# Seven products instead of eight for the seventh down chunk of two MLPs, with the recombination spread over VectorE and accumulating transfers

## What is computed

```python
h = rms_norm(x, norm_mlp[l])
x = x + jnp.square(jax.nn.relu(h @ w_up[l])) @ w_down[l]      # first block
return rms_norm(x, norm_final)

hid = jnp.square(jax.nn.relu(jnp.einsum('bsd,df->bsf', n2, w_up[l])))   # second block
mlp_out = jnp.einsum('bsf,fd->bsd', hid, w_down[l])
h = h + rms_norm_2(mlp_out, norm_mlp_post[l])
```

## Time and profile before

| | |
|---|---|
| three runs | 1566.63, 1567.47, 1567.72 us, median 1567.47 |
| the profiled execution | 1567.51 us, of which span 1565.7 us |
| granted TensorE clock | 0.999 |
| TensorE matmuls busy | 1549.0 us, 99% of the span, 7752 instructions |
| VectorE, ScalarE, GpSimd busy | 987.3, 662.7, 482.6 us |

### The profile page before, as it was taken

The page is one execution under the profiler, slowest core; times in us unless marked ns, Lnnn a source line. Parts: engine busy times, 40 slices in busy tenths (PEclk is TensorE's granted clock), DMA queues, the critical chain, the costliest instruction groups (busy, mean ns, idle before and its releaser), DMA issues.

```text
span 1565.7 us, 21038 instructions
## 1 busy us (share of the span) xinstructions
PE 1549.0 (99%) x7752; PEld 1303.1 (83%) x7752; DVE 987.3 (63%) x1188; ACT 662.7 (42%) x1092; POOL 482.6 (31%) x282
## 2 busy tenths in 40 slices
PE   8999999999999999999999999999999999999998
PEld 6888888888788888888888898988888988888886
DVE  5454876435477776876664747357356677777765
ACT  5352665244444443443533433643334453434342
POOL 2451000000037776752300000020013047767732
PEclk9999999999999999999999999999999999999999
DMA  6422136221313233215332132243334332213133
GB/s 247 150 70 79 41 108 191 79 81 54 135 54 108 108 108 107 107 55 160 89 106 83 55 95 71 92 162 105 111 124 147 135 108 102 89 45 135 67 116 120
DMA packets 44997, 164.35 MB, mean 105 GB/s; under 512 B 5584, under 2 KB 5784, under 8 KB 44272
## 3 DMA queue, kind: packets, MB, share of 16 engines
q1 hardware_dynamic: 40608, 144.82, 28.4%
q0 software_dynamic: 4304, 18.38, 3.4%
HBM read 158.89 MB, written 5.85 MB: 105 GB/s over the span
## 4 chain that ended last, share of the span: by engine, by line
PE 93%; DVE 4%; ACT 2%; DMA 1%; issue 1%; SPq 0%; DVEq 0%; ACTq 0%
PE banks L1235 29%; PE banks L1237 29%; PE banks L1236 29%; PE banks L1534 1%; PE banks L1413 1%; DVE nmax L2230 1%; DVE w_lo L1944 1%; DMA w_raw<-in_weights 1%; PE banks L1352 0%; PE banks L1596 0%; DVE banks L2229 0%; PE banks L1572 0%; PE banks L1564 0%; PE banks L1523 0%; DMA x_tok<-in_x 0%
## 5 line engine op out<-in xcount | busy, mean ns | idle before, releaser
L1235 PE MATMUL banks<-act_hi,w_hi 128*128 128x512 f32 (+1 forms) x1088 | 413.7, 380 | 3.1 <-DVE act_lo L2112 3.1
L1237 PE MATMUL banks<-act_hi,w_lo 128*128 128x512 f32 (+1 forms) x1088 | 410.3, 377 | 0.0
L1236 PE MATMUL banks<-act_lo,w_hi 128*128 128x512 f32 (+1 forms) x1088 | 410.2, 377 | 0.0
L1944 DVE TENSOR_TENSOR w_lo<-w_raw,w_hi 128x1024 fp32r<-128x1024 f32 x216 | 280.0, 1303 | 203.2 <-ACT w_hi L1632 199.8
L1632 ACT ACTIVATE w_hi<-w_raw 128x1024 fp32r<-128x1024 f32 x216 | 227.0, 1059 | 251.6 <-DMA w_raw<-in_weights 196.8
L1235 PEld LDWEIGHTS banks<-act_hi,w_hi 128*128 128x128 f32 x1088 | 204.9, 188 | 40.8 <-DVE w_lo L1944 1.6
L1237 PEld LDWEIGHTS banks<-act_hi,w_lo 128*128 128x128 f32 x1088 | 204.9, 188 | 37.7
L1236 PEld LDWEIGHTS banks<-act_lo,w_hi 128*128 128x128 f32 x1088 | 205.0, 188 | 36.4
L1235 PE MATMUL banks<-w_hi,a_hi 128*128 128x512 f32 x400 | 155.8, 389 | 0.0
L1237 PE MATMUL banks<-w_hi,a_lo 128*128 128x512 f32 x400 | 155.7, 389 | 0.0
L1236 PE MATMUL banks<-w_lo,a_hi 128*128 128x512 f32 x400 | 155.7, 389 | 0.0
(11 more groups left out here) (367 smaller groups left out, 2393.4 us busy)
## 6 DMA issues: line engine op xcount, KB each, us to landing
w_raw<-in_weights SPq DMA_DIRECT2D x216, 512.0 KB, 3.7
w_down<-in_weights SPq DMA_DIRECT2D x48, 512.0 KB, 6.4
wide<-share_dram POOLq DMA_DIRECT2D x3, 1024.0 KB, 10.2
x_tok<-in_x SPq DMA_DIRECT2D x4, 512.0 KB, 5.2
w_first<-in_weights SPq DMA_DIRECT2D x4, 512.0 KB, 8.5
x_tok<-in_x POOLq DMA_DIRECT2D x4, 512.0 KB, 5.0
x_dram<-x_tok POOLq DMA_DIRECT2D x1, 2048.0 KB, 8.1
x_tok<-x_dram POOLq DMA_DIRECT2D x1, 2048.0 KB, 8.5
```

The lines of the kernel that those rows point to most:

```text
L1235: pe.matmul(out_ap, lhs[0], rhs[0], start=start, stop=False)
L1236: pe.matmul(out_ap, lhs[0], rhs[1], start=False, stop=False)
L1237: return pe.matmul(out_ap, lhs[1], rhs[0], start=False, stop=stop)
L1944: dve.tensor_tensor(w_lo[:, slot, :], landed(kind, raw), w_hi[:, slot, :], ALU.subtract).then_inc(lo_w, 1)
```

## The change

Chunk 6 of both networks is done by seven products as well (`seven`, `last=True`), with banks 4, 6, 0, 2, 4, 6, 2 (and each one's neighbour) instead of 4 and 6 in turn. Its weights come through `w_down`, and POOL makes their block sums in up 7. The step `whole` (`sq` to `act_hi`, `act_lo` for chunk 7) moves ahead of the products; the replaced part is gone. The recombination leaves up 7: in the product stage VectorE does q6 += q1 after product 2, q7 += q6 after product 4, x12 += q6 and x12 += q5 after product 5; x21 += q7 comes right ahead of VectorE's add of tile 2, half 0, of chunk 7. The quarters x11 (+= q1) and x22 (+= q5, += q7) are left to accumulating transfers from SBUF to SBUF, 512 KB each, that POOL issues; POOL itself waits for the q5 transfer before it issues the q7 one. `load2` keeps six of its transfers and moves behind product 6's evacuation; the seventh (`row2`) is issued after product 0. The return of x in the second block goes to a buffer of its own, `x_late`, from product 0 on. VectorE waits for the transfers at tile 0 half 0 and at tile 2 half 1.

```diff
-    return name in ("w_down", "w_down_2") and row0 < FF - 2 * T
+    return name in ("w_down", "w_down_2") and row0 < FF - T
...
+        if last:
+            sums, held = None, self.count("lo_a", 4)
+            self.add("whole", held=held, sq=squared)
...
-            bank = 4 + 2 * (j % 2)
+            bank = (4, 6, 0, 2, 4, 6, 2)[j] if last else 4 + 2 * (j % 2)
...
-        s.add("whole", held=s.count("lo_a", 1), sq=s.count("sq", 0), dst="parts")
-        up(after="fold")
-        after_last()
-        steps = s.bank_steps("add", "tok", "parts", rows=4, halves=2, dst=dst)
-        go(steps, 1)
-        s.add("whole", held=s.count("lo_a", 4), sq=s.count("sq", 0), dst="act")
-        go(steps, 16)
-        s.add("unpark", ready=ready(), dst=dst)
+        up()
+        for st in s.products(dst, last=True):
+            taken = filled_by(st)
+            if st.n == 0:
+                first_out(taken)
+                s.add("unpark", ready=taken, dst=dst)
+            s.add("fold", n=st.n, ready=taken, dst=dst)
+        after_last(taken)
         last(s.bank_steps("add", "tok", "act", rows=4, halves=2, dst=dst, by_tile=True))
...
-    run_mlp("x", lambda: s.add("load2", ready=all_out()), first_end)
+    run_mlp("x", lambda taken: s.add("row2_load", ready=taken), lambda taken: s.add("load2", ready=taken), first_end)
...
             def fold(st):
...
+                q, (x11, x12, x21, x22) = sums_of[st.dst], quarters(st.dst)
+                if st.n > 0:
+                    wait_ready(dve, st.ready, None)
+                if st.n == 2:
+                    then(dve.tensor_tensor(q["q6"], q["q6"], q["q1"], ALU.add))
+                elif st.n == 4:
+                    dve.tensor_tensor(q["q7"], q["q7"], q["q6"], ALU.add).then_inc(q7_made, 1)
+                    dve.wait_ge(q7_made, FOLDED[st.dst] // 16)
+                elif st.n == 5:
+                    then(dve.tensor_tensor(x12, x12, q["q6"], ALU.add))
+                    then(dve.tensor_tensor(x12, x12, q["q5"], ALU.add))
...
+            def fold_late(dst):
...
+                x21 = quarters(dst)[2]
+                then(dve.tensor_tensor(x21, x21, sums_of[dst]["q7"], ALU.add))
...
+                    if st.rows == 4:
+                        for name in {(0, 0): ("x11",), (2, 1): ("x22_q5", "x22")}.get((st.nth, st.half), ()):
+                            dve.wait_ge(fold_in[name], FOLDED[st.dst])
                     part = dst[:, st.nth, col0:col0 + 512]
+                    if st.rows == 4 and (st.nth, st.half) == (2, 0):
+                        fold_late(st.dst)
...
+            def fold_by_dma(st):
...
+                if st.n in (1, 3):
+                    wait_ready(pool, st.ready, None)
+                if st.n == 1:
+                    pool.dma_start(x11, q["q1"], accum_op=ALU.add).then_inc(fold_in["x11"], 16)
+                elif st.n == 3 and st.dst == "y":
+                    pool.dma_start(x22, q["q5"]).then_inc(fold_in["x22_q5"], 16)
+                elif st.n == 3:
+                    pool.dma_start(x22, q["q5"], accum_op=ALU.add).then_inc(fold_in["x22_q5"], 16)
+                elif st.n == 4:
+                    pool.wait_ge(q7_made, done // 16)
+                    pool.wait_ge(fold_in["x22_q5"], done)
+                    pool.dma_start(x22, q["q7"], accum_op=ALU.add).then_inc(fold_in["x22"], 16)
```

More of the change, by code:

```diff
@@ L374, in ahead, with products @@
         return out
-    def products(self, dst, first=False):
+    def products(self, dst, first=False, last=False):
         g = self.group
@@ L387, in products @@
         squared = self.count("sq", 0)
-        sums = self.add("sums", counts={"sum_a": 4}, sq=squared, held=self.count("lo_a", 0)).sum_a
-        held = self.count("lo_a", 7)
+        if last:
+            sums, held = None, self.count("lo_a", 4)
+            self.add("whole", held=held, sq=squared)
+        else:
+            sums = self.add("sums", counts={"sum_a": 4}, sq=squared, held=self.count("lo_a", 0)).sum_a
+            held = self.count("lo_a", 7)
         for j in range(7):
-            bank = 4 + 2 * (j % 2)
+            bank = (4, 6, 0, 2, 4, 6, 2)[j] if last else 4 + 2 * (j % 2)
             banks = (bank, bank + 1)
@@ L398, in products @@
             ends.append((bank + 1, self.cell(self.fills[bank + 1] + 1, ("bank", bank + 1))))
-            yield self.add("product", banks, n=j, dst=dst, first=first, splits=splits,
+            yield self.add("product", banks, n=j, dst=dst, first=first, last=last, splits=splits,
                            units=[self.placed(self.mine[j])], held=held, of=ends, sum_a=sums, sq=squared)
-        self.last_bank = 5
+        self.last_bank = bank + 1
 def at(count, turn, plus=0):
@@ L1042, in two_blocks @@
         tile_done = sem("tile_done")
-        fold_made, parked, x_again = sem("fold_made"), sem("parked"), sem("x_again")
+        parked, x_again = sem("parked"), sem("x_again")
+        fold_in = {name: sem(f"fold_{name}") for name in ("x11", "x22_q5", "x22")}
+        q7_made = sem("q7_made")
         sq_made = sem("sq_made")
@@ L1152, in part_lo, with quarters @@
             eng.tensor_tensor(a_lo[:, j], parts[j], a_hi[:, j], ALU.subtract).then_inc(lo_a, 1)
+        def quarters(dst):
+            rows_of = {"x": x, "y": y}[dst]
+            return [rows_of[:, 2 * rows:2 * rows + 2, 512 * cols_:512 * cols_ + 512] for rows in range(2) for cols_ in range(2)]
         def copies_of(st):
@@ L1716, in handle @@
                     split(st, turn)
+                    if st.last:
+                        return
                     act.wait_ge(sq_made, at(st.sq, turn))
@@ L2030, in handle @@
                     split(st, turn)
+                elif k == "fold":
+                    fold(st)
                 elif k == "product":
@@ L2400, in handle @@
                     block_sums(pool, st, turn)
-                elif k == "product":
+                elif k == "product" and not st.last:
                     for j in (st.n - 1, st.n) if st.n == 6 else (st.n - 1,):
@@ L2405, in handle @@
                 elif k == "whole":
-                    pool.wait_ge(hi_a, at(st.held, turn, 1))
-                    if st.dst == "parts":
-                        pool.tensor_tensor(a_lo[:, 2], sq[:, 0:2, low_], a_hi[:, 2], ALU.subtract).then_inc(lo_a, 1)
-                    else:
-                        for c in range(4):
-                            pool.wait_ge(hi_a, at(st.held, turn, c + 1))
-                            pool.tensor_tensor(act_lo[:, c, :], sq[:, c, :], act_hi[:, c, :], ALU.subtract).then_inc(lo_a, 1)
+                    for c in range(4):
+                        pool.wait_ge(hi_a, at(st.held, turn, c + 1))
+                        pool.tensor_tensor(act_lo[:, c, :], sq[:, c, :], act_hi[:, c, :], ALU.subtract).then_inc(lo_a, 1)
+                elif k == "fold":
+                    fold_by_dma(st)
                 elif k == "gemm":
@@ L2467, in handle @@
                     if st.mode == "final":
-                        pool.wait_ge(fold_made, 1)
+                        for name in {0: ("x11",), 1: (), 2: ("x22_q5",), 3: ("x22",)}[st.n]:
+                            pool.wait_ge(fold_in[name], 16)
                     src = x if st.mode == "final" else y
@@ L2514, in handle @@
                         pool.dma_start(wide[p][:].rearrange("q t h -> q (t h)"), share_dram[p].partition_broadcast(P)).then_inc(wide_in[p], 16)
+            def fold_by_dma(st):
+                q, (x11, x12, x21, x22) = sums_of[st.dst], quarters(st.dst)
+                done = FOLDED[st.dst]
+                if st.n in (1, 3):
[10 more added lines that the diff above has]
+                    pool.dma_start(x22, q["q7"], accum_op=ALU.add).then_inc(fold_in["x22"], 16)
             def level(n, st):
```

51 lines of the change are left out of this document (17 added, 34 removed).

## The result

| | before | after |
|---|---|---|
| median | 1567.19 us | 1570.72 us |
| lowest and highest of 22 runs each | 1566.63 to 1568.02 | 1568.68 to 1572.42 |
| profiled execution, span | 1567.51, 1565.7 us | 1570.68, 1568.9 us |
| granted TensorE clock over the span | 0.999 | 0.997 |

The ratio is 1.0022, 95% interval 1.0016 to 1.0028: 3.5 us slower, where 1.2 us faster than these 1567.19 was predicted. It lies above the range (1569.4), so this is a miss.

What follows compares the result with a forecast made beforehand. TensorE's matmuls fill 99% of the span and bound the kernel. Against 1567.51 us: -5.44 saved, +2.7 first turn, +0.5 second turn, +0.7 at the end, -1.5 in sum, 1566.0 us; range 1563.2 to 1569.4.

Steps and rivals of the forecast that it cites:

- The saving: Chunk 6's product stages: 84 matmuls where the plain chunk has 96, saving 2.72 us per block, 5.44 in all.
- the third rival: Product stage: late loads make TensorE wait for bank 2, losing the saving there too; 1569.5 or 1567.8 us, chance 0.15.
- VectorE's backlog: Chunk 6's product stage: VectorE some 4 us behind when down 7 begins, evacuating product 6 at t near 22.3 to 23.5.
- The place of the damage: First block: six `load2` issues hold POOL from 23.5 to 26.7, ahead of its first work on tile 0.
- The x21 term: Addition at tile 2 of chunk 7: 0.5 us at the first block's second turn, 0.7 us at the program's end.
- The second block: Forecast change of the second block's time: -2.0 us.
- What the delay does in the first block: First turn, tile 0: late `load2` issues make TensorE wait 3.4 us for `h_tok`, 2.7 us added.
- I take 6.2: Accumulating 512 KB transfers between SBUF buffers: 6.2 us each, between 5.0 from below and 8.5 from above.
- the prediction's own sign: On POOL in the new profile: a wait for the q5 transfer past t = 24 would mean the second rival.
- the second rival: Slow accumulating transfers hold POOL ahead of `load2` and tile 0: 1570 us at 10.5 us each, 1574 at 12.5; chance 0.15.

Runs made afterwards that it cites:

- e10: First block as before the change, second block changed, with its x21 addition moved into the product stage behind product 6: 1564.53 us, ratio 0.9983 to before.
- e3: First block as before the change, second block as in the changed kernel: 1564.95 us, ratio 0.9986 to before.
- e8: Changed kernel with the first block's three accumulating transfers as plain copies of the same bytes: 1570.16 us, ratio 1.0017 to before.
- e1: Changed kernel with the six `load2` transfers issued behind tile 0's first addition instead of ahead of it: 1567.39 us, ratio 1.0000 to before.
- e7: Changed kernel with 22 useless matmuls (5.0 us) ahead of the first block's first turn: 1568.66 us, ratio 1.0007 to before.
- e9: e1 with 14 useless matmuls (3.2 us) ahead of the first turn: 1565.94 us, ratio 0.9993 to before.
- e2: Changed kernel with VectorE adding q7 to q5 and one transfer to x22 in place of two: 1571.51 us, ratio 1.0028 to before.
- e4: Changed kernel with the x21 addition in the product stage, behind product 6, in both blocks: 1569.87 us, ratio 1.0016 to before.
- e6: e5 with the second block's x21 addition moved behind product 6's evacuation: 1568.24 us, ratio 1.0008 to before.
- e5: e1 with tile 0 of the first block turned one half tile later, behind tile 2's first half: 1568.81 us, ratio 1.0012 to before.

## Why the prediction was wrong

**What held.** The saving: both product stages of 19.04 us, no gap, no wait for banks or weights; the third rival did not come. VectorE's backlog: product 6 evacuated at t = 23.0 to 24.3 (said: 22.3 to 23.5), three late loads and four additions being its content. The place of the damage: six issues in front of tile 0's product. The x21 term: 0.5 us at the second turn (0.52 measured), 0.7 at the end (0.76; e10 takes it away). The second block: -2.0 said, -2.2 measured alone (e3).

**The step that failed is "What the delay does in the first block", the sum of which was 2.7 us.** The path was right (six issues of `load2` ahead of tile 0's product) and its size was not. The wait was 5.8 us, not 3.4. Worked along the chain: the issues of `load2` were to start at t = 23.5 and started at 25.5, of which 0.7 is product 6 done later than said, 0.6 GpSimd still held by q5 until t = 24.8, and 0.7 the q7 issue, which the sum had behind other work. The six issues took 3.3 instead of 3.2: tile 0's product at 28.9, not 26.7. It took 1.73 us instead of 1.29. Together 2.6 us later, and from the end of that product to the turn it took 5.3 us, as said (28.05 to 33.3).

Within that step the term "I take 6.2" was mis-sized: 8.4 to 8.9 were measured, at the upper bound of 8.5. The value came from loads out of DRAM, 5.0 us each, and e8 shows that a copy from SBUF in that place takes 6.9 even without accumulating. By the prediction's own sign (GpSimd waiting for q5 past t = 24) the second rival is what happened, and its chance of 0.15 was too small. That its 1570 lies near the measured 1570.7 is luck: it belongs to a transfer of 10.5 us, and for 8.9 its rule puts the landing at 23.8 and leaves the price under 1 us. Nor does the transfer alone carry the loss: with it 1.5 us shorter (e8) only 0.6 us came back, inside the spread, since product 6's evacuation stands right beside it. The six issues do more: put behind one addition (e1), they gave back 3.3 us.

**And a term stood at nothing: the granted clock.** The prediction counted a wait of TensorE as its length alone, without a reason. e7 and e9 show what that leaves out: 2.1 us behind a wait of 5.8, and 1.45 behind one of 3.3, both got back by matmuls of no use while the wait itself stayed as long. By the medians the first block's part of the change costs 5.8 us (the changed kernel against e3), where +0.5 was forecast. Of the 5.3 between, 2.6 are the longer wait (5.26 against 2.7) and 2.1 the clock; 0.6 is left over, within what single runs differ by. In the profiled execution the clock cost 1.4 us; in those of e2 and e4, with nearly the same wait, the low stretch was 6.8 us long instead of 3.4 and reached from inside the wait to behind it, at a cost of 1.8 and 2.2 us. That fits the wider spread of the changed kernel (3.7 us from lowest to highest, against 1.4 before); this link is argued, not shown.

**Left open.** What it would take to win in the first block. With the issues moved and the wait filled (e9) the changed kernel is 1.2 us faster than before, at the edge of what its interval can tell from nothing, and still 1.0 slower than e3, which leaves that block alone. So there the scheme's 2.7 us are still spent, on VectorE's backlog of some 4 us and on the q5 transfer, which end within 0.2 us of each other. Taking away only one of them was tried (e2, e8) and gained nothing clear; a version without either was not tried.

## What to carry to other kernels

Price a new wait of the busiest engine twice: its length, and the slow stretch behind it if the granted clock falls; in this kernel the second was 1.4 to 2.2 us on a wait of 3 to 6. Before moving issues of DMAs, ask whose first urgent work stands behind them in the same queue: moving six cheap issues gave back 3.3 us, shortening the transfer that looked dangerous by 1.5 us gave 0.6. Where two engines are late at nearly the same time, taking away one delay gains only the distance to the other. And the same edit can win in one block and lose in another: where nothing feeds TensorE behind the stage it brought 2.2 of the 2.7 us (2.6 with the x21 addition moved), where a norm and a turn follow at once the block came out 5.8 us longer.

## What the runs showed of the hardware

- Accumulating transfers from SBUF to SBUF of 512 KB took 8.7, 8.4 and 7.3 us from issue to landing in the first block, and 12.8 (beside the 2 MB return of x) and 5.0 (at a DMA share of 0.61) in the second, where q5 is copied and not added, in 9.0. Plain copies of the same bytes, in e8, took 6.9, 6.9 and 3.1 us in the places of the first three. The Trainium skill, "Collectives: The Full Stack", section "The bandwidth ceiling: the fold count and why AG ≠ RS ≠ AR", says of the ReduceScatter of a ring that its add needs two source reads and halves the rate. Here the whole transfers took 1.2 to 1.3 times as long in the first two places, beside the same loads. That is less than double, but it counts a whole transfer with whatever is fixed in it, so it decides nothing on the rate.
- Issuing such a transfer held GpSimd for 0.70 us (741.48 to 742.18), where loads follow each other at 0.53. Accumulating is not the reason: the rows of e8's copies are 0.71 to 0.75 us long.
- The granted clock went to its lower level, 1.2 GHz, on waits of a TensorE that was otherwise fully busy: inside the waits of 4.75 (e8), 5.23 (e2), 5.66 (e4) and 5.79 us, and behind those of 3.27 (e1), 2.97 (e6) and even 1.86 and 1.41 us (e5, the second with 0.41 us behind it). It did not fall on the 1.88 us of e6, on the 0.71 us of e7, nor on the 0.53 us of before. So the length of the wait alone does not settle it. It stayed low for 3.4 us in some executions and for about 6.8 in others, and the longer stretch did not go with the longest wait (5.79 us, 3.4).
